# Four feed-forwards without riders: one 512-column matmul of the high weights against both parts of h, corrections summed on VectorE

## The reference

```python
def _swiglu(x, w_in, w_out):
    gate, up = jnp.split(x @ w_in, 2, axis=-1)
    return (jax.nn.silu(gate) * up) @ w_out
```

## Time and profile before

| | |
|---|---|
| median of 3 runs | 2502.56 us (2501.92 to 2503.19) |
| span of the profiled execution, first to last instruction | 2502.1 us, which is 0.5 us under the median; its time with what lies around the span is not listed apart, and the runs bound it at 2501.92 to 2503.19 us |
| TensorE matmuls, busy | 2374.3 us (95%), 19576 of them |
| TensorE weight loads, busy | 2222.4 us (89%), 19576 |
| VectorE, busy | 1670.2 us (67%) |
| ScalarE, busy | 1186.4 us (47%) |
| DMA | 481.63 MB, mean 192 GB/s |
| mean granted TensorE clock | 0.991 of full speed |

### The profile page before, as it was taken

The page is one execution under the profiler, slowest core; times in us unless marked ns, Lnnn a source line. Parts: engine busy times, 40 slices in busy tenths (PEclk is TensorE's granted clock), DMA queues, the critical chain, the costliest instruction groups (busy, mean ns, idle before and its releaser), DMA issues.

```text
span 2502.1 us, 50249 instructions
## 1 busy us (share of the span) xinstructions
PE 2374.3 (95%) x19576; PEld 2222.4 (89%) x19576; DVE 1670.2 (67%) x2657; ACT 1186.4 (47%) x1779; POOL 12.2 (0%) x28
## 2 busy tenths in 40 slices
PE   4999999999999889999999998999999999999998
PEld 4998989989999768998999998899999999888998
DVE  6777977777788766666556575665565575856555
ACT  4445354453444565445446563554454465636443
POOL 0000000000000000000000000000000000000000
PEclk9999999999999999999999999999999999999999
DMA  8886868867788314664555342455555553404553
GB/s 327 285 282 218 288 250 284 282 214 280 262 311 307 113 52 153 205 220 156 187 183 180 122 130 68 137 173 185 185 169 185 184 169 110 151 30 160 193 186 123
DMA packets 130450, 481.63 MB, mean 192 GB/s; under 512 B 14608, under 2 KB 14656, under 8 KB 129776
## 3 DMA queue, kind: packets, MB, share of 16 engines
q1 hardware_dynamic: 128448, 468.36, 55.4%
q0 software_dynamic: 1840, 10.93, 1.2%
HBM read 478.15 MB, written 1.07 MB: 192 GB/s over the span
## 4 chain that ended last, share of the span: by engine, by line
PE 52%; issue 35%; DVE 5%; ACT 5%; DMA 2%; POOL 0%; DVEq 0%; SPq 0%; ACTq 0%; POOLq 0%
PE bank L565 51%; ACT w_hi L1333 2%; DMA ring<-weights 1%; DVE w_lo L1912 1%; ACT work L1333 1%; ACT sq L1333 1%; PE bank L596 1%; DVE y L1946 1%; ACT L1333 1%; DMA rows<-row 0%; PE bank L1149 0%; DVE work L2372 0%; DVE sq L2721 0%; DVE work L2719 0%; DVE work L2161 0%
## 5 line engine op out<-in xcount | busy, mean ns | idle before, releaser
L1912 DVE TENSOR_TENSOR w_lo<-ring,w_hi 128x1024 fp32r<-128x1024 f32 x715 | 870.7, 1223 | 586.8 <-ACT w_hi L1333 580.9
L565 PE MATMUL bank<-h_hi,w_hi 128*128 128x256 f32 x3896 | 1117.3, 287 | 32.2 <-DVE w_lo L1912 16.5
L1333 ACT ACTIVATE w_hi<-ring 128x1024 fp32r<-128x1024 f32 x726 | 764.8, 1057 | 789.5 <-PE bank L565 712.2
L565 PE MATMUL bank<-h_lo,w_hi 128*128 128x256 f32 x3896 | 1106.8, 284 | 0.0
L565 PE MATMUL bank<-h_hi,w_lo 128*128 128x256 f32 x3896 | 1106.5, 284 | 0.0
L565 PEld LDWEIGHTS bank<-h_hi,w_hi 128*128 128x128 f32 x3896 | 751.1, 193 | 46.4 <-issue 26.4
L565 PEld LDWEIGHTS bank<-h_lo,w_hi 128*128 128x128 f32 x3896 | 751.3, 193 | 3.5
L565 PEld LDWEIGHTS bank<-h_hi,w_lo 128*128 128x128 f32 x3896 | 750.8, 193 | 0.1
L565 PE MATMUL bank<-w_hi,act_hi 128*128 128x512 f32 x704 | 275.0, 391 | 0.0
L565 PE MATMUL bank<-w_lo,act_hi 128*128 128x512 f32 x704 | 274.9, 391 | 0.0
L565 PE MATMUL bank<-w_hi,act_lo 128*128 128x512 f32 x704 | 273.9, 389 | 0.0
(11 more groups left out here) (216 smaller groups left out, 1746.5 us busy)
## 6 DMA issues: line engine op xcount, KB each, us to landing
ring<-weights SPq DMA_DIRECT2D x886, 512.0 KB, 4.8
work<-cmp POOLq DMA_DIRECT2D x1, 4096.0 KB, 14.2
sq<-rows POOLq DMA_DIRECT2D x6, 512.0 KB, 6.4
work<-lora POOLq DMA_DIRECT2D x2, 1024.0 KB, 5.0
x<-x_in SPq DMA_DIRECT2D x1, 1024.0 KB, 11.4
out<-y SPq DMA_DIRECT2D x2, 512.0 KB, 2.6
const_sb<-consts SPq DMA_DIRECT2D x1, 854.0 KB, 13.0
const_sb<-consts POOLq DMA_DIRECT2D x1, 726.0 KB, 7.2
```

Source lines behind the costliest of these rows:

```text
L565: return nc.tensor.matmul(out, lhsT, rhs, start=start, stop=stop, skip_group_check=skip)
L1333: return nc.scalar.activation(out, in_, f, bias=bias, scale=scale, **kw)
L1912: tt(w_lo[q % SLOTS][:, :], ring[n % RING][:, c * HALF:(c + 1) * HALF], w_hi[q % SLOTS][:, :].bitcast(F32), ALU.subtract).then_inc(halves_ ...
```

## The change

In the four feed-forwards without riders, for blocks hh = 1 to 20:

- h_hi and h_lo become two views of one buffer, `h_split`, and `h_both[:, k]` is the high and the low columns of block k as one 512-column operand in two pieces, 2048 elements apart.
- `gate_up_apart` replaces `gate_up`: per k and half, one matmul of 256 columns (low weights by h_hi) into the second half of a bank, and one of 512 columns (high weights by h_both) into the whole bank. So the first 256 columns of the bank hold high by high, the second 256 the two corrections. Gate and up have a bank each, and odd and even blocks take turns between banks 6, 7 and banks 4, 5.
- ScalarE copies the correction columns of both banks to SBUF (one 128x512 operation); VectorE adds them to the high-by-high columns (one 128x512 operation, into `summed`). The silu reads `summed`, as does the product of silu and up.
- New semaphores: `corr_copied` (ScalarE to VectorE), `sides_summed` (VectorE to ScalarE, and to TensorE, which waits for the sum of block hh - 2 before it writes the same banks), `hidden_made`. `front_taken` now counts only blocks 0 and 21 of these feed-forwards.
- Block 0 keeps the old form in bank 4 or 5, block 21 the old form in bank 6.
- ScalarE's list for a step becomes: copy(odd), split q+6, silu(odd), split q+7, copy(even), split q+8, silu(even), splits q+9 to q+11. VectorE's becomes: sum(odd), low part q+6, three operations (odd), low part q+7, sum(even), low part q+8, three operations (even), low parts q+9 to q+11.

```diff
-        h_hi, h_lo = sb("h_hi", KC * TOK, F32R), sb("h_lo", KC * TOK, F32R)
+        h_split = sb("h_split", 2 * KC * TOK, F32R)
+        h_hi, h_lo = h_split[:, 0:KC * TOK], h_split[:, KC * TOK:2 * KC * TOK]
...
+        h_both = h_split[:, :].rearrange("p (e j t) -> p j e t", e=2, j=KC)
...
+        corr, summed = carve(0, 2, 2, TOK), carve(1024, 2, 2, TOK)
+
+        def sides(hh):
+
+            return (6, 7) if hh % 2 else (4, 5)
...
+        def both_banks(hh):
+
+            b = sides(hh)[0]
+            return banks[:, b * 512:(b + 2) * 512].rearrange("p (g e t) -> p g e t", g=2, e=2)
...
+            def gate_up_apart(st, q, hh, turn=0):
+
+                if hh == 2:
+                    pe.wait_ge(front_taken, st.front + 1)
+                elif hh > 2:
+                    pe.wait_ge(sides_summed, turn * 2 + (st.apart + hh - 2))
+                for i in range(2):
+                    half_wait(q + i, turn * 6)
+                    w, b = (q + i) % SLOTS, sides(hh)[i]
+                    for k in range(KC):
+                        mm(half(b, 1), wlo3[w][:, k, :], hi3[:, k, :], k == 0, False, True)
+                        ins = mm(pair(b), whi3[w][:, k, :], h_both[:, k], False, k == KC - 1, True)
+                    ins.then_inc(half_used, 1)
...
-                    gate_up(st, q + 6 * s + 2, 2 * s + 1, turn)
-                    gate_up(st, q + 6 * s + 4, 2 * s + 2, turn)
+                    (gate_up if st.riders else gate_up_apart)(st, q + 6 * s + 2, 2 * s + 1, turn)
+                    (gate_up if st.riders else gate_up_apart)(st, q + 6 * s + 4, 2 * s + 2, turn)
...
-                gate_up(st, q + 6 * FFN_STEPS - 4, HALVES - 1)
+                gate_up(st, q + 6 * FFN_STEPS - 4, HALVES - 1, to=None if st.riders else sides(HALVES - 1)[0])
...
+                def corrections(hh, j, turn):
+                    act.wait_ge(half_used, turn * 6 + (q + j + 1))
+                    fn(corr[:, hh % 2], both_banks(hh)[:, :, 1], ACT.Copy).then_inc(corr_copied, 1)
+
+                def gate_apart(hh, turn):
+                    act.wait_ge(sides_summed, turn * 2 + (st.apart + hh))
+                    fn(silu_t[:, silu_at(st, hh)], summed[:, hh % 2, 0], ACT.Silu).then_inc(silu_ready, 1)
...
-                        gate(1, 3, turn)
+                        corrections(1, 3, turn)
                         hi(q + 6, turn)
+                        gate_apart(1, turn)
                         hi(q + 7, turn)
-                        gate(2, 5, turn)
-                        for i in range(8, 12):
+                        corrections(2, 5, turn)
+                        hi(q + 8, turn)
+                        gate_apart(2, turn)
+                        for i in range(9, 12):
                             hi(q + i, turn)
...
+                def sum_sides(hh, turn):
+                    dve.wait_ge(corr_copied, turn * 2 + (st.apart + hh))
+                    tt(summed[:, hh % 2], corr[:, hh % 2], both_banks(hh)[:, :, 0], ALU.add).then_inc(sides_summed, 1)
+
+                def gated_apart(hh, turn, slot_free):
+                    h = HALVES * st.ffn + hh
+                    a = slice(hh % 2 * TOK, (hh % 2 + 1) * TOK)
+                    dve.wait_ge(silu_ready, turn * 2 + (h + 1))
+                    tt(act_t[:, a], silu_t[:, silu_at(st, hh)], summed[:, hh % 2, 1], ALU.mult
+                       ).then_inc(hidden_made, 1)
+                    dve.wait_ge(half_used, turn * 6 + slot_free)
...
-                        gated(1, turn, q + 2)
+                        sum_sides(1, turn)
                         lo(q + 6, turn)
+                        gated_apart(1, turn, q + 2)
                         lo(q + 7, turn)
+                        sum_sides(2, turn)
                         lo(q + 8, turn)
-                        gated(2, turn, q + 7)
+                        gated_apart(2, turn, q + 7)
                         lo(q + 9, turn)
```

## The result

The changed kernel took 2495.89 us (median of 6 runs, 2494.27 to 2498.47) against 2503.36 us for the kernel before in runs beside it (2501.92 to 2508.38): a ratio of 0.9966, 95% interval 0.9955 to 0.9977. It is faster: the medians lie 7.5 us apart, and the ratio, which does not go by the two medians alone, stands for 0.34% or 8.5 us, where 17.0 us were forecast. The profiled execution took 2495.58 us, with a span of 2493.6 us, 8.5 us under the span of before.

What follows compares the result with a forecast made beforehand. TensorE's matmul spacing was taken to pace the feed-forward loops. 1280 pairs at 13.3 ns saved give 17.0 us, other engines, DMA and banks nothing: 2502.6 - 17.0 = 2485.6 us, with an 8-in-10 range of 2477 to 2494.

Steps and rivals of the forecast that it cites:

- 1280 pairs: Gate/up matmuls in four feed-forwards: three of 256 columns become one of 256 and one of 512, saving 17.0 us.
- fixed part of 13.3 ns: TensorE time each matmul pays beyond its columns, at either width; one such part goes per pair.
- I take 346.7: Gate/up price of one 256-column plus one 512-column matmul: 120.0 + 226.7 = 346.7 ns, against 360 ns before.
- upper bound of 351.7: Dearest price in the bounds for a gate/up pair, 120 + 231.7 ns, leaving 10.6 us saved.
- bad end of the range: Dear side of the pair's price: 351.7 ns, 10.6 us saved; at worst 240 ns per 512-column matmul, zero gain.
- sign of being wrong: In the loops: 512-column matmul not within some 5 ns of 227, or TensorE idle time released by a low part.
- (b): Gate/up: overhead grows with h's columns, or the second piece costs a fixed part; nothing saved, 2502.6 us; chance 8%.
- (c): Gate/up: second operand piece restarts the stream at 26.7 ns, 253 ns per 512-column matmul, 2519.6 us; chance 3%.
- ScalarE and VectorE at nothing: Loop steps: added copies (1.2 us) and sums (1.4 us) cost no time, covered by 2.3 us to spare.
- (d): Loops: split chain late beyond its 2.3 us, TensorE waits twice a step; 0.5 us each give 2526 us; chance 2%.
- The downs "stay": The 24 down matmuls of 512 columns per step keep their form and time, 227.9 ns each.
- The base: Starting time of the sum: the kernel before's median, 2502.56 us, 0.5 over the profiled span of 2502.1 us.

Runs made afterwards that it cites:

- groups of two: Changed kernel issuing two 256-column matmuls, then two of 512, and so on: ratio 0.9939 to the kernel before, span 2482.3 us, step 16.59 us.
- contiguous operand: Changed kernel with h's high and low columns of a block side by side, so the 512-column matmul reads one piece: ratio 0.9951 to the kernel before, step 16.79 us.
- mirrored order: Changed kernel with eight wide matmuls before eight narrow in the first weight half, behind them in the second: median 2487.44 us, ratio 0.9927 to the kernel before.
- the kernel with doubled work: Changed kernel with ScalarE's correction copy and VectorE's sum each issued twice: one run, span 2495.4 us, step 16.79 us.
- groups of four: Changed kernel issuing four 256-column matmuls, then four of 512, and so on: one run, span 2489.4 us, step 16.69 us.
- grouped: Changed kernel issuing, per weight half, eight 256-column matmuls, then eight of 512: ratio 0.9925 to the kernel before, step 16.61 us; with contiguous layout too, 0.9935.

## Why the prediction was wrong

- **What bounds, and where it counts: right.** TensorE's spacing is the whole of a step before and after; no wait took its place.
- **1280 pairs, one matmul less in each: right** (19576 to 18296), and the fixed part of 13.3 ns is real among equal widths: the step is a sum of 120.0 and 226.7 ns wherever widths don't mix.
- **The step that failed** is "I take 346.7: the switch rows show 115 in one direction and about 232 in the other, which together are 346.7 too". The pair measured 353.3 ns, so 6.7 were saved instead of 13.3, and it lay above even the upper bound of 351.7. Both figures were read behind lone switches, after which equal widths follow. The sum took it that they hold when every matmul is a switch, and nowhere in the trace of before do the two widths take turns like that. They don't hold there: the intervals repeat as 113, 233, 117, 241, 120, 236 ns. That a switch costs something net did stand in the rows: the first six 512s behind 256s had 231.7 ns each, 30 ns more in sum, against 10 ns won back on two 256s (7 in the unrounded starts, 114 and 119 ns). I took that series for the bad end of the range only. But it does not give 353 either, and it gave 350.5 for the groups of two, where 348.3 was measured. The prediction's own sign of being wrong, a wide matmul not within some 5 ns of 227, came out: it took 236.7. 6.7 x 1280 is 8.6 us; less 0.02 us a step lost on the downs (0.8 us in 40), that leaves 7.8, and with the two short intervals of each old step, which go too (7 ns a step, 0.3 us), the loops' 7.5 us.
- **The two-piece operand**, on which the bad end of the range and rivals (b) and (c) were built: costs nothing (contiguous operand). Rival (b)'s other half, an overhead that grows with h's columns, falls as well: behind its like, the wide matmul over both parts of h settles at 226.7 ns (the first half of the mirrored order), as the weights do.
- **ScalarE and VectorE at nothing: right**, with 2.7 us to spare (2.4 forecast); the kernel with doubled work confirms it, and no wait came up, so (d) falls. Copy 597 and sum 687 ns, as priced.
- **The downs "stay": off by a little.** They take 5.49 us behind pairs, 5.47 behind groups of four, 5.44 behind groups of two and eight and the mirrored ones, and took 5.47 before.
- **The base: 0.8 us low.** The sum starts at 2502.6 us, the median of three runs; with the runs beside the changed kernel it is 2503.36. The miss of 10.3 us (2495.89 against 2485.6) is this 0.8 and 9.5 us of gain that did not come (17.0 forecast, 7.5 between the medians). The 0.5 us between span and median did not enter, since 17.0 was taken off the median. In every later run the time is 1.8 to 3.2 us over the span, so the profiled execution of before, with its span of 2502.1 us, was perhaps none of the three; its time is not known.

The Trainium skill (TensorE: Matmul & The Clock Gate, Back-to-back issue gap) gives the isolated gap of a matmul by its own width alone, as the columns' time plus about 2.5 ns at the full clock. Here, with a weight load before every matmul, equal widths do have one gap each, but a larger one (13.3 ns over the columns in the loops), and a mixed stream is not the sum of them: 353 ns where 120.0 + 226.7 would be 346.7.

## What to carry to other kernels

In a loop like this one, paced by TensorE with a weight load before every matmul, merging two narrow matmuls saves the whole fixed part (13.3 ns here) only where equal widths stand together; in turns one by one, half of it was lost. Let equal widths be neighbours, across the borders of groups too, and measure the group's length: longer was not always better here. If a change makes every instruction a transition that the rows show only alone, they don't price it: neither the settled intervals nor the first ones behind a lone switch (113 + 233 = 346 ns) gave the 353. Say that no row has the stream, and widen the range by the net cost of a lone switch (30 - 10 = 20 ns by the rows, which would have held 353). The extra copies and sums, on engines with 2.7 us to spare, cost nothing, and issuing them twice was a cheap way to show it.

## What the runs showed of the hardware that was not expected

Matmuls of 256 and 512 columns in turn repeat with a period of three pairs, 1.06 us, and not of one. The cost of a step is the same for a contiguous and a two-piece operand, for overlapping and separate banks, and for either order in the pair. Groups of two are nearly as good as the mirrored order (348.3 and 347.9 ns a pair), and groups of four are worse (350.7). The reason stays open. A moving operand in two pieces 2048 elements apart streams as fast as a contiguous one (a step of 16.79 us with either, 16.61 with either when grouped).
